# Second block of a four-layer model on one core: where the embedding sums go, how far the expert tiles are fetched ahead, when the router is split, and how the gate's bias is added

## The chip, the cores and the metric

The kernel runs on one core of one Trainium2 chip. The metric is the time of one execution on the device, in microseconds. Engines are called by their names: TensorE (PE in the rows, its weight loads PEld), VectorE (DVE), ScalarE (ACT), GpSimd (POOL) and SyncE (SP), which only issues DMAs here.

## What is computed

512 tokens of width 1024 pass two layers of a first block (not touched by the change) and two layers of a second one. A layer of the second block is, in the reference's own code:

```python
x = layer_norm(DEEPNORM_ALPHA * x + mix @ w_o[i], ln1_g[i], ln1_b[i])
ffn = expert_choice_moe(x, router_w[i], w1[i], w3[i], w2[i])
ple = jax.nn.sigmoid(x @ ple_gate_w[i] + ple_gate_b[i]) * (p[i] @ ple_w[i])
x = layer_norm(DEEPNORM_ALPHA * x + ffn + ple, ln2_g[i], ln2_b[i])
```

`expert_choice_moe` takes a softmax of `x @ router_w` over 16 experts; each expert picks its 64 best tokens, gathers their rows of x, computes `(silu(xg @ w1) * (xg @ w3)) @ w2`, weighs the result by the affinity and adds it to the token's row. One expert's three matrices are 1024x1024 floats each.

## The kernel before, in words

Products that need more than one rounded pass are written as three: an operand is split into `hi` (rounded to fp32r, by ScalarE) and `lo` (the rest, by VectorE), and `products` gives hi x hi, hi x lo, lo x hi. Some products stay whole in f32.

`gemm` is the stage that all projections use. It runs over weight tiles of 128x2048 floats (1 MB), four of which lie in a ring (`w_ring`); each is split into `pl_w_hi` and `pl_w_lo` in one of two homes, and each has its outputs, numbered k through the stage. A stage can have a `lead`, here the transposes of x into `xT` (32 on TensorE, then ScalarE's `xT_hi` and VectorE's `xT_lo`, eight each), and a `side`: work that each engine does ahead of its output k. Each engine runs its own list in order and waits on semaphores; a stage ends with a barrier of all engines.

A layer of the second block has, after its mixer, two stages:

- The embedding stage (`pl`, built by `ple_tiles`). Outputs 0 to 15 are the gate `x @ ple_gate_w`: four 1 MB tiles, each with four outputs of twelve products; a bank gets two of them, and at the end of the second (outputs 4 to 7 and 12 to 15) one more product adds the bias: row n of an identity, spread over 128 columns, times `pb`, whose two rows are the bias. ScalarE then writes the sigmoid into `pg`. Outputs 16 to 23 are `p @ ple_w`, six products each; VectorE multiplies by `pg` and scales x by 1.41 and adds to it, in two instructions. The side is `route_beside`, the routing. TensorE: logits ahead of output 1 (24 products with the split router `rws`), transposes ahead of 2, 4, 11 and 13, the gather of the first two experts' tokens ahead of 18 and 20. VectorE: the router's split (`split_router`) ahead of its output 0, softmax at 1, the top-64 search at 3 and 4, the places at 7. SP: router weights, an iota table, `pb`, six expert tiles into `ex_front`, and after the places the p rows, then the embedding weight. ScalarE copies x to `xs` at its output 0, because the gather reads it while VectorE changes x; VectorE waits for that at output 16.
- The experts stage (`experts`). Two experts are taken in one turn, eight turns of 24 tiles: 8 of w1, 8 of w3, 8 of w2. The tiles go round twelve slots, four of the ring, six of `ex_front`, two of `ex_back`; the last two belong to this stage alone, so SP fetches them at its start. After that SP refills a slot when TensorE is done with its tile. The first ten are there when the stage begins. Each expert's result is scattered by products, and VectorE adds it to x; the layer norm follows.

In `gemm`, VectorE's list begins so (ScalarE's has the same form), and it is here that the change moves an entry:

```python
split(0)
...
for n in range(len(tiles)):
    for m in ahead_of(n):
        split(m)
    for k in range(last[n] - len(outs_of[n]), last[n]):
        if side and k in side.dve:
            side.dve[k](dve, s)
```

so the second weight tile is split ahead of whatever the side does at output 0.

Of the kernel before, what the change touches and what calls it, by code (L numbers as in the profile page):

```python
# [44 lines left out]
DEPTH = 2  # L45

# [165 lines left out]
def gemm(nc, label, ps, ring, tiles, pre=0, nxt=(), lead=None, also=(), side=None, banks=NB):  # L212
# [10 lines left out]
    with ExitStack() as ctx:  # L223
# [43 lines left out]
        with stage(nc, label, f"{names} {side.names}" if side else names, clear=ready) as (block, s):  # L267
# [136 lines left out]
            def _(dve):  # L404
# [1796 lines left out]
def route_beside(nc, ctx, ps, C, x, xT, pt, pT, pb, I, iota, pos, aff_s, xs, E, i):  # L2201
# [7 lines left out]
    mx, work, top = sb("mx", [P, 3, TT]), sb("work", [NE, 2, T]), sb("top", [NE, 8, 8])  # L2209
# [5 lines left out]
    def sp(sp, s):  # L2215
# [3 lines left out]
        sp.dma_start(pb[:, :], I["ple_gate_b_2"][i].rearrange("(a n) -> a n", a=2)).then_inc(s.pb_in, 16)  # L2219
# [6 lines left out]
    def pool(pool, s):  # L2226
        pool.memset(ones[:, :], 1.0).then_inc(s.ones, 1)
# [4 lines left out]
    def bias_in(pe, s):  # L2232
        pe.wait_ge(s.pb_in, 16)
# [72 lines left out]
    def split_router(dve, s):  # L2306
# [3 lines left out]
        dve.tensor_tensor(rws.lo[:, :, :], rw[:, :, :], rws.hi[:, :, :].bitcast(F32), ALU.subtract).then_inc(s.rw_split, 1)  # L2310

# [81 lines left out]
def gather(pe, ps, bank, xs, E, j):  # L2393

    for t in range(TT):
        mm = pe.matmul(ps[:, bank + j // 4, j % 4 * P:j % 4 * P + P], xs[:, t, pairs_of(j)], E.sel_now[:, t, :], start=(t == 0), stop=(t == TT - 1))  # L2396
# [8 lines left out]
def experts(nc, ps, ring, C, w1, w3, w2, x, xs, iota, pos, aff_s, E, i, gain, bias, store=None, nxt=()):  # L2405
# [15 lines left out]
    with ExitStack() as ctx:  # L2421
        def sb(name, shape, dt=F32):
            return ctx.enter_context(sbuf(nc, f"{name}{i}", shape, dt))
        back = sb("ex_back", [P, BACK, SLOT])
# [14 lines left out]
        slots = RING + AHEAD + BACK  # L2439

        def slot(n):
            n = n % slots
            home, first = (ring.slots, 0) if n < RING else (E.front, RING) if n < RING + AHEAD else (back, RING + AHEAD)
# [15 lines left out]
        with stage(nc, f"ex{i}", names, clear=ready) as (block, s):  # L2459
# [5 lines left out]
            def _(sp):  # L2465
# [11 lines left out]
                for m in range(RING + AHEAD, slots):  # L2477
                    fetch(0, m)
# [35 lines left out]
            def _(pe):  # L2514
                def gather_next(js):
                    for j in js:
                        mm = gather(pe, ps, H1_BANK, xs, E, j)
# [82 lines left out]
            def _(act):  # L2600
# [25 lines left out]
                def total(t):  # L2626
                    act.wait_ge(s.added, (turns - 1) * SC + 2 * t + 2)
                    act.activation(junk[:, t, :], x[:, t, :], ACT.Copy, accum_out=col(SUM, t)).then_inc(s.n_sum, 1)
                total(0)
                for t in range(TT):  # L2630
# [3 lines left out]
                    act.activation(junk[:, t, :], x[:, t, :], ACT.Square, bias=col(LESS_MEAN, t), accum_out=col(SQUARES, t)).then_inc(s.n_squares, 1)  # L2634
# [4 lines left out]
            def _(dve):  # L2639
# [42 lines left out]
                def centre(t):  # L2682
                    dve.scalar_tensor_tensor(y[:, t, :], x[:, t, :], col(LESS_MEAN, t), rows[:, 0, :], ALU.add, ALU.mult).then_inc(s.n_less, 1)
# [18 lines left out]
def ple_tiles(I, i, xT, pT, pb, C, x, pg):  # L2702


    def gate(w, n, q, t):
# [6 lines left out]
        mm.append((C.ident[0:2, n:n + 1].broadcast_to([2, P]), pb[0][:, :]))  # L2712
        return out(P, 512, mm, bank=bank, first=False, **to(pg[0][:, t, cols], "A", 1.0, ACT.Sigmoid))

    def embed(w, hf, t):
        cols = slice(512 * hf, 512 * hf + 512)

        def v(e, p, st):
            g = pg[0][:, t, cols]
# [3 lines left out]
            return e.scalar_tensor_tensor(x[:, t, cols], x[:, t, cols], ALPHA, g, ALU.mult, ALU.add)  # L2723
# [7 lines left out]
def block2_layer(nc, ps, ring, C, x, I, i, store, nxt):  # L2731
    late = {n: [] for n in ("xT", "pT", "pb", "pg")}
    ple = ple_tiles(I, i, late["xT"], late["pT"], late["pb"], C, x, late["pg"])
# [12 lines left out]
    with ExitStack() as ctx:  # L2746
        def sb(name, shape, c=ctx):
            return c.enter_context(sbuf(nc, f"{name}{i}", shape, F32))

        xs = sb("xs", [P, TT, D])  # L2750
# [5 lines left out]
                  ready=[ctx.enter_context(nc.semaphore(f"ex{i}_ready{n}")) for n in range(AHEAD + BACK)], order=[I[n][i] for n in ("w1_2", "w3_2", "w2_2")])  # L2756
        with ExitStack() as c2:
            xT, pT = pair(nc, c2, f"xT{i}", [P, DC, T]), pair(nc, c2, f"pT{i}", [P, 2, T])
            pg, pb = sb("pg", [P, TT, D], c2), sb("pb", [2, 512], c2)
            for n, tensor in (("xT", xT), ("pT", pT), ("pg", pg), ("pb", pb)):  # L2760
# [111 lines left out]
```

## Time and profile before

| | us |
|---|---|
| median of three runs | 3378.24 |
| lowest and highest | 3373.71 and 3387.47 |
| the profiled execution, its own time | 3375.86 |
| its span, first to last instruction | 3374.1 |

The profile is that of one execution. Times in its rows count from the span's start. In the timeline a row gives start, duration, engine, line, operation, what it writes and reads, and in brackets how long the engine had been idle and what released it; "x4" is four instructions merged in one row. SPq rows are DMA issues. Layer 0 of the second block has its embedding stage from 1973.3 and its experts stage from 2066.2; in layer 1 these are 2798.7 and 2892.0.

### The profile page before, as it was taken

The numbers are of one execution on the slowest core, as the hardware profiler recorded it, in microseconds if no ns is written. First come the engines' busy times: TensorE is split into PE (matmuls) and PEld (weight loads), VectorE is DVE, ScalarE is ACT, GpSimd is POOL, SyncE is SP. The second block draws the span as 40 slices with busy tenths as digits, with TensorE's granted clock in tenths as the row PEclk, the third lists the DMA queues.
The fourth block names the chain that finished last, engine by engine and source line by source line (L and its number), as shares of the span: only waits on it lengthen the run. The fifth ranks groups of instructions, "written<-read, shape, count | busy, mean of one in ns | idle before, by whom it ended". The sixth has DMA issues, their size and how long they took to land. (4 is left out here: it accounts for less than half of the span.)

```text
span 3374.1 us, 39981 instructions
## 1 busy us (share of the span) xinstructions
PE 3186.6 (94%) x16110; PEld 2169.8 (64%) x16110; DVE 1285.4 (38%) x1773; ACT 957.7 (28%) x1570; POOL 236.3 (7%) x361
## 2 busy tenths in 40 slices
PE   7999999999999999999997999999988899999996
PEld 5886578888787667888785566444437456544442
DVE  4425554242532564334366462111116655111113
ACT  3325433142422633323343421010013543000001
POOL 1004200000100410000000200000000310000000
PEclk9998999999999999999998999999998999999998
DMA  5310123231441022323311136999992113799997
GB/s 159 119 56 26 63 82 99 95 99 63 131 138 38 1 88 88 100 89 99 91 37 43 68 119 254 426 427 426 427 415 64 58 63 134 303 426 427 427 427 303
DMA packets 234295, 590.22 MB, mean 175 GB/s; under 512 B 42962, under 2 KB 146328, under 8 KB 184996
## 3 DMA queue, kind: packets, MB, share of 16 engines
q1 hardware_dynamic: 234148, 588.15, 46.0%
q8 instruction: 105, 1.72, 0.2%
q14 instruction: 42, 0.34, 0.0%
HBM read 581.81 MB, written 2.10 MB: 173 GB/s over the span
## 5 line engine op out<-in xcount | busy, mean ns | idle before, releaser
L2576 PE MATMUL ps<-w_ring,xe 128*64 128x512 f32 x1024 | 233.8, 602 | 18.5 <-DMA w_ring<-in_w 13.4
L422 DVE TENSOR_TENSOR mlp_w_lo<-w_ring,mlp_w_hi 128x2048 fp32r<-128x2048 f32 x62 | 142.1, 2292 | 205.7 <-ACT mlp_w_hi L382 205.7
L357 PE MATMUL ps<-h_hi,in_w_hi 128*128 128x512 f32 (+1 forms) x528 | 206.9, 392 | 2.6 <-DVE h_lo L430 2.6
L357 PE MATMUL ps<-h_lo,in_w_hi 128*128 128x512 f32 (+1 forms) x528 | 205.6, 389 | 0.0
L357 PE MATMUL ps<-h_hi,in_w_lo 128*128 128x512 f32 (+1 forms) x528 | 205.6, 389 | 0.0
L357 PE MATMUL ps<-h_hi,mlp_w_hi 128*128 128x512 f32 x512 | 199.4, 389 | 2.0 <-DVE h_lo L430 2.0
L357 PE MATMUL ps<-h_hi,mlp_w_lo 128*128 128x512 f32 x512 | 199.2, 389 | 0.0
L357 PE MATMUL ps<-h_lo,mlp_w_hi 128*128 128x512 f32 x512 | 199.2, 389 | 0.0
L357 PE MATMUL ps<-mlp_w_lo,u_hi 128*128 128x512 f32 x512 | 199.2, 389 | 0.0
L357 PE MATMUL ps<-mlp_w_hi,u_hi 128*128 128x512 f32 x512 | 199.2, 389 | 0.0
L357 PE MATMUL ps<-mlp_w_hi,u_lo 128*128 128x512 f32 x512 | 199.2, 389 | 0.0
L382 ACT ACTIVATE mlp_w_hi<-w_ring 128x2048 fp32r<-128x2048 f32 x62 | 118.5, 1911 | 230.1 <-PE ps L357 230.1
L2576 PEld LDWEIGHTS ps<-w_ring,xe 128*64 128x64 f32 x1024 | 75.6, 138 | 164.5 <-issue 164.4
L2576 PE MATMUL ps<-ex_front,xe 128*64 128x512 f32 x768 | 174.4, 598 | 0.0
L2576 PE MATMUL ps<-ex_front,hidT 128*64 128x512 f32 x768 | 168.8, 594 | 2.5 <-ACT hidT L2616 2.2
L2667 DVE SCALAR_TENSOR_TENSOR ye_lo<-ps,g_now,ye_hi 128x1024 fp32r<-128x1024 f32 x16 | 20.5, 1284 | 354.1 <-ACT ye_hi L2622 354.1
L2647 DVE TENSOR_TENSOR x<-x,ps 128x512 f32<-128x512 f32 x128 | 82.2, 683 | 169.3 <-PE ps L2539 169.3
L422 DVE TENSOR_TENSOR in_w_lo<-w_ring,in_w_hi 128x2048 fp32r<-128x2048 f32 (+1 forms) x38 | 83.4, 2194 | 133.3 <-ACT in_w_hi L382 133.1
L2396 PEld LDWEIGHTS ps<-sel_now,xs 128*128 128x128 f32 x1024 | 123.5, 196 | 11.7 <-issue 11.4
L2396 PE MATMUL ps<-sel_now,xs 128*128 128x128 f32 x1024 | 127.2, 283 | 0.0
L700 ACT ACTIVATE w_ring<-ps,at_top 128x128 f32<-128x128 f32 (+1 forms) x192 | 99.2, 523 | 98.2 <-DVE at_top L757 98.0
L2576 PEld LDWEIGHTS ps<-ex_front,hidT 128*64 128x64 f32 x768 | 54.0, 137 | 105.3 <-issue 101.0
(551 smaller groups left out, 6146.1 us busy)
## 6 DMA issues: line engine op xcount, KB each, us to landing
ex_front<-in_w SPq DMA_DIRECT2D x192, 1024.0 KB, 17.4
w_ring<-in_w SPq DMA_DIRECT2D x128, 1024.0 KB, 20.5
ex_back<-in_w SPq DMA_DIRECT2D x64, 1024.0 KB, 19.7
w_ring<-in_w_in SPq DMA_DIRECT2D x32, 1024.0 KB, 5.4
w_ring<-in_w_up SPq DMA_DIRECT2D x32, 1024.0 KB, 5.4
w_ring<-in_w_down SPq DMA_DIRECT2D x32, 1024.0 KB, 5.0
w_ring<-in_cmp_w SPq DMA_DIRECT2D x16, 512.0 KB, 4.9
w_ring<-in_w_out SPq DMA_DIRECT2D x8, 1024.0 KB, 6.1
```

The lines of the kernel that those rows point to most:

```text
L357: mm = pe.matmul(ps[0:o.rows, bank[k], 0:o.cols], lhsT, rhs, start=(o.first and j == 0), stop=(o.final and j == len(o.mm) - 1))
L382: act.activation(w.hi[:, home(n), 0:used], ring.slots[:, n % RING, 0:used], ACT.Copy).then_inc(s.hi_done, 1)
L422: dve.tensor_tensor(w.lo[:, home(n), 0:used], ring.slots[:, n % RING, 0:used], w.hi[:, home(n), 0:used].bitcast(F32), ALU.subtract).then_i ...
L700: act.activation(probs[:, u % (LAG + 1), a, 0:n], ps[:, S_BANK + 2 * (u % 2) + a, 0:n], ACT.Exp, bias=top[:, u % 8, a:a + 1], accum_out=to ...
L2396: mm = pe.matmul(ps[:, bank + j // 4, j % 4 * P:j % 4 * P + P], xs[:, t, pairs_of(j)], E.sel_now[:, t, :], start=(t == 0), stop=(t == TT - 1))
L2576: mm = pe.matmul(ps[rows, bank + half, :], lhsT, slot(2 * m + a)[:, kk, 512 * half:512 * half + 512], start=(k == 0), stop=(k == DC - 1))
L2647: dve.tensor_tensor(d, d, ps[:, TR_BANK + n % 2 if bank is None else bank, :], ALU.add).then_inc(s.added, 1)
L2667: dve.scalar_tensor_tensor(ye.lo[:, :], ps[:, Y_BANK:Y_BANK + 2, :].rearrange("p b n -> p (b n)"), g_now[:, :], ye.hi[:, :].bitcast(F32), ...
```

## The change

`LEAD` is a new place in the side's list of VectorE: after the lead's remainders and before any further tile is split. `split_router` moves there. The bias becomes a product in fp32r: `pb` is now 128 rows, zeroed by GpSimd, with the rounded bias in rows 0 and 1 (ScalarE, `round_bias`) and what the rounding left in rows 32 and 33 (VectorE, `rest_of_bias`); the stationary side is a column of `marks`, the rounded form of a table that has ones in rows n, 32 + n, 64 + n and 96 + n. TensorE waits for it ahead of output 4. `pg` is gone: gates, embedding sums and the experts' adds use one buffer `acc`, so x stays as it was until the layer norm, the gather reads x, and `xs`, its copies and the wait for them go. `ex_back` is gone too: `ex_front` has eight tiles, all fetched in the embedding stage.

```diff
+LEAD = -1
@@ gemm, VectorE
+                if side and LEAD in side.dve:
+                    side.dve[LEAD](dve, s)
                 for n in range(len(tiles)):
@@ route_beside
-    mx, work, top = sb("mx", [P, 3, TT]), sb("work", [NE, 2, T]), sb("top", [NE, 8, 8])
+    mx, tables, top = sb("mx", [P, 3, TT]), sb("work", [P, 2, T]), sb("top", [NE, 8, 8])
+    work, pb_in = tables[0:NE, :, :], tables[HD:HD + LO + 2, 0, :]
...
-        sp.dma_start(pb[:, :], I["ple_gate_b_2"][i].rearrange("(a n) -> a n", a=2)).then_inc(s.pb_in, 16)
+        for r in (0, LO):
+            sp.dma_start(pb_in[r:r + 2, :], I["ple_gate_b_2"][i].rearrange("(a n) -> a n", a=2)).then_inc(s.pb_in, 16)
         for m in range(AHEAD):
...
+        pool.memset(pb[:, :].bitcast(F32), 0.0).then_inc(s.pb_zero, 1)
...
     def bias_in(pe, s):
-        pe.wait_ge(s.pb_in, 16)
+        pe.wait_ge(s.pb_lo, 1)
...
             if b == 0:
                 pe.wait_ge(s.selected, 1)
-                pe.wait_ge(s.x_kept, TT)
...
-                mm = gather(pe, ps, ROUTE_A, xs, E, j)
+                mm = gather(pe, ps, ROUTE_A, x, E, j)
...
-    def keep_x(act, s):
-        for t in range(TT):
-            act.activation(xs[:, t, :], x[:, t, :], ACT.Copy).then_inc(s.x_kept, 1)
+    def round_bias(act, s):
+        act.wait_ge(s.pb_in, 32)
+        act.wait_ge(s.pb_zero, 1)
+        for r in (0, LO):
+            ins = act.activation(pb[r:r + 2, :], pb_in[r:r + 2, :], ACT.Copy)
+        ins.then_inc(s.pb_hi, 1)
...
+    def rest_of_bias(dve, s):
+        dve.wait_ge(s.pb_hi, 1)
+        dve.tensor_tensor(pb[LO:LO + 2, :], pb_in[LO:LO + 2, :], pb[LO:LO + 2, :].bitcast(F32), ALU.subtract).then_inc(s.pb_lo, 1)
...
-    return beside(names, sp, {0: bias_in, 1: logits_by_expert, 2: logits_by_token, 4: affinities_by_expert, 11: places_by_token, 13: p_by_feature, 16: p_ready, 18: gather_half(0), 20: gather_half(1)},
-                  {0: keep_x, 3: exponentials, 14: round_p, 20: take_half(0), 22: take_half(1)},
-                  {0: split_router, 1: softmax, 3: take_top(0, 3), 4: take_top(3, 8), 7: places, 11: keep_places, 14: rest_of_p, 15: select_first, 16: x_is_kept}, pool)
+    return beside(names, sp, {1: logits_by_expert, 2: logits_by_token, 4: bias_and_affinities, 11: places_by_token, 13: p_by_feature, 16: p_ready, 18: gather_half(0), 20: gather_half(1)},
+                  {0: round_bias, 3: exponentials, 14: round_p, 20: take_half(0), 22: take_half(1)},
+                  {LEAD: split_router, 0: rest_of_bias, 1: softmax, 3: take_top(0, 3), 4: take_top(3, 8), 7: places, 11: keep_places, 14: rest_of_p, 15: select_first}, pool)
 
-AHEAD, BACK = 6, 2
+AHEAD = 8
@@ experts
-        slots = RING + AHEAD + BACK
+        slots = RING + AHEAD
...
-                for m in range(RING + AHEAD, slots):
-                    fetch(0, m)
                 with sp.Fori(0, turns - 1) as it:
@@ ple_tiles
-        mm.append((C.ident[0:2, n:n + 1].broadcast_to([2, P]), pb[0][:, :]))
-        return out(P, 512, mm, bank=bank, first=False, **to(pg[0][:, t, cols], "A", 1.0, ACT.Sigmoid))
+        mm.append((C.marks[:, n:n + 1].broadcast_to([P, P]), pb[0][:, :]))
+        return out(P, 512, mm, bank=bank, first=False, **to(acc[0][:, t, cols], "A", 1.0, ACT.Sigmoid))
...
-            return e.scalar_tensor_tensor(x[:, t, cols], x[:, t, cols], ALPHA, g, ALU.mult, ALU.add)
+            return e.scalar_tensor_tensor(g, x[:, t, cols], ALPHA, g, ALU.mult, ALU.add)
@@ block2_layer
-        xs = sb("xs", [P, TT, D])
+        acc = sb("acc", [P, TT, D])
...
-            pg, pb = sb("pg", [P, TT, D], c2), sb("pb", [2, 512], c2)
+            pb = c2.enter_context(sbuf(nc, f"pb{i}", [P, 512], F32R))
@@ build, the stage that rounds the tables at the start
-                for dst, src in ((C.ident_r[:, :], C.ident[:, :]), (C.later[:, :], tri), (C.cmp_neg[:, :, :], cmp)):
+                for dst, src in ((C.ident_r[:, :], C.ident[:, :]), (C.later[:, :], tri), (C.marks[:, :], C.heads), (C.cmp_neg[:, :, :], cmp)):
                     act.activation(dst, src, ACT.Copy).then_inc(s.copied, 1)
```

In the lists below, line numbers of the changed kernel are a few higher than before, since lines were added. VectorE, start of layer 0's embedding stage, before: the split of the first tile, the eight remainders of xT, the second tile, the router, the copy of the logits (into `p`) and the softmax's first steps.

```order
L414 TENSOR_TENSOR pl_w_lo<-w_ring,pl_w_hi 128x512 x4
L430 SCALAR_TENSOR_TENSOR xT_lo<-ps,xT_hi 128x512 x8
L422 TENSOR_TENSOR pl_w_lo<-w_ring,pl_w_hi 128x2048
L2308 CAST rws_hi<-rw_448 128x128
L2310 TENSOR_TENSOR rws_lo<-rw_448,rws_hi 128x128
L2315 COPY p_435<-ps 16x512
L2317 COPY lg_449<-ps 128x64
```

The same place in the changed kernel:

```order
L415 TENSOR_TENSOR pl_w_lo<-w_ring,pl_w_hi 128x512 x4
L431 SCALAR_TENSOR_TENSOR xT_lo<-ps,xT_hi 128x512 x8
L2316 CAST rws_hi<-rw_448 128x128
L2318 TENSOR_TENSOR rws_lo<-rw_448,rws_hi 128x128
L423 TENSOR_TENSOR pl_w_lo<-w_ring,pl_w_hi 128x2048
L2322 TENSOR_TENSOR pb_447<-work_451,pb_447 2x512
L2327 COPY p_436<-ps 16x512
L2329 COPY lg_449<-ps 128x64
```

The router's two instructions now stand ahead of the second tile's split, and the bias remainder stands between that split and the copy of the logits.

SP, from the bias of layer 0 to the first refill in the experts stage, before (the ISA and branch rows are the barrier and the stage's loop):

```order
L2219 DMA pb_447<-in_ple_gate_b 2x512
L2222 DMA ex_front_433<-in_w_2 128x2048 x6
L2224 DMA p_435<-in_p 128x4x256
L292 DMA w_ring<-in_ple_w 128x2x1024
L302 DMA w_ring<-in_w_2 128x2048 x4
L115 UNCONDITIONAL_BRANCH
L118 ISA x5
L2464 UNCONDITIONAL_BRANCH
L2470 DMA ex_back_498<-in_w_2 128x2048 x2
```

and in the changed kernel, where `work` is the buffer that also holds the bias as it arrives:

```order
L2224 DMA work_451<-in_ple_gate_b 2x512 x2
L2227 DMA ex_front_434<-in_w_2 128x2048 x8
L2229 DMA p_436<-in_p 128x4x256
L293 DMA w_ring<-in_ple_w 128x2x1024
L303 DMA w_ring<-in_w_2 128x2048 x4
L116 UNCONDITIONAL_BRANCH
L119 ISA x5
L2476 UNCONDITIONAL_BRANCH
```

Two expert tiles moved from the experts stage's start into the run of front tiles, and the bias is fetched twice.

ScalarE, the same start, before: two rounds of tile splits around the transposes of x, then the copies of x, then the exponentials.

```order
L372 ACTIVATE pl_w_hi<-w_ring 128x512 x4
L389 ACTIVATE xT_hi<-ps 128x512 x8
L382 ACTIVATE pl_w_hi<-w_ring 128x2048
L2295 ACTIVATE xs_432<-x 128x1024 x4
L2299 ACT_TABLE_LOAD
L2299 ACTIVATE lg_449<-lg_449 128x64
```

and in the changed kernel:

```order
L373 ACTIVATE pl_w_hi<-w_ring 128x512 x4
L390 ACTIVATE xT_hi<-ps 128x512 x8
L383 ACTIVATE pl_w_hi<-w_ring 128x2048
L2302 ACTIVATE pb_447<-work_451 2x512 x2
L2307 ACT_TABLE_LOAD
L2307 ACTIVATE lg_449<-lg_449 128x64
```

The four copies are replaced by the two roundings of the bias.

## Rows read from the trace of the kernel before

**Rows 1.** The page: span.

```profile
span 3374.1 us, 39981 instructions
```

**Rows 2.** Windows of both experts stages: busy time, then PEclk, DMA share, GB/s.

```profile
2066.20:2071.95 5.75, 5.53 (x18) 2.07 (x20) 0.00 (x0) 1.28 (x1) 0.19 (x1) 0.70 0.81 302
2071.95:2493.20 421.25, 416.33 (x2136) 189.16 (x2132) 60.83 (x93) 35.54 (x44) 2.46 (x13) 1.00 1.01 426
...
2940.00:3319.60 379.60, 374.22 (x1906) 168.14 (x1904) 58.61 (x89) 31.82 (x39) 2.09 (x11) 1.00 1.01 427
```

**Rows 3.** Timeline of layer 0's experts stage, SP and TensorE.

```profile
2066.22 0.80 SPq L2470 DMA_DIRECT2D ex_back<-in_w  x2
2071.95 4.32 SPq L2470 DMA_DIRECT2D w_ring<-in_w  x4
...
2518.18 3.65 PE L2576 MATMUL ps<-ex_back,hidT 128*64 128x512 f32 x16 [1.28 <-DMA ex_back<-in_w]
```

**Rows 4.** Timeline of layer 0, around the logits.

```profile
1976.41 4.87 DVE L430 SCALAR_TENSOR_TENSOR xT_lo<-ps,xT_hi 128x512 fp32r<-128x512 f32 x8
...
1981.50 0.39 PE L357 MATMUL ps<-pl_w_hi,xT_lo 128*128 128x512 f32 x1
...
1983.99 0.22 DVE L2308 CAST rws_hi<-rw 128x128 fp32r<-128x128 f32 x1
1984.24 0.29 DVE L2310 TENSOR_TENSOR rws_lo<-rw,rws_hi 128x128 fp32r<-128x128 f32 x1
...
1984.68 0.58 PE L2240 MATMUL ps<-xT_hi,rws_hi 128*16 128x512 f32 x1 [2.79 <-DVE rws_lo L2310]
...
1991.70 0.40 PE L357 MATMUL ps<-pl_w_hi,xT_hi 128*128 128x512 f32 x1
```

**Rows 5.** Timeline of layer 1, the same place.

```profile
2801.75 4.87 DVE L430 SCALAR_TENSOR_TENSOR xT_lo<-ps,xT_hi 128x512 fp32r<-128x512 f32 x8
...
2807.19 0.39 PE L357 MATMUL ps<-pl_w_hi,xT_lo 128*128 128x512 f32 x1
...
2810.30 0.39 PE L2240 MATMUL ps<-xT_hi,rws_hi 128*16 128x512 f32 x1 [2.73 <-DVE rws_lo L2310]
...
2817.41 0.40 PE L357 MATMUL ps<-pl_w_hi,xT_hi 128*128 128x512 f32 x1
```

**Rows 6.** Windows of TensorE alone: length, busy (instructions), granted clock, DMA share, GB/s.

```profile
1975.00:1977.00 2.00, 2.00 (x11) 0.50 0.81 158
...
1979.00:1981.73 2.73, 2.73 (x14) 1.00 1.02 429
...
1984.68:1988.01 3.33, 3.33 (x9) 0.51 1.02 431
1988.01:2003.80 15.79, 15.79 (x74) 1.00 0.20 85
```

**Rows 7.** Timeline of layer 0: gates on ScalarE, embedding sums on VectorE.

```profile
2012.91 0.60 ACT L467 ACTIVATE pg<-ps 128x512 f32<-128x512 f32 x1 [3.39 <-PE ps L357]
2016.90 0.60 ACT L467 ACTIVATE pg<-ps 128x512 f32<-128x512 f32 x1 [3.39 <-PE ps L357]
...
2062.58 0.69 DVE L2722 TENSOR_TENSOR pg<-ps,pg 128x512 f32<-128x512 f32 x1
...
2063.94 0.69 DVE L2722 TENSOR_TENSOR pg<-ps,pg 128x512 f32<-128x512 f32 x1
```

**Rows 8.** Timeline: ScalarE's copies, GpSimd's memset, a rounding at the program's start.

```profile
12.70 0.29 ACT L2789 ACTIVATE cmp_neg<-w_ring 128x128 fp32r<-128x128 f32 x1
...
1973.32 0.52 POOL L2227 MEMSET p<- 16x512 f32 x1 [65.73 <-POOLq L119]
...
1981.61 3.91 ACT L2295 ACTIVATE xs<-x 128x1024 f32<-128x1024 f32 x4
```

**Rows 9.** Timeline of layer 0: last step of the places, their transposes.

```profile
2018.47 0.42 DVE L2346 TENSOR_SCALAR work<-work 16x512 f32<-16x512 f32 x1
...
2025.18 0.42 PE L2258 MATMUL ps<-ident,work 16*128 16x16 f32 x4
```

More of the change, by code:

```diff
@@ L2390, in select, with gather @@
                              E.pos_now[:, :, :].unsqueeze(3).broadcast_to(shape), ALU.is_equal)
-def gather(pe, ps, bank, xs, E, j):
+def gather(pe, ps, bank, x, E, j):
     for t in range(TT):
-        mm = pe.matmul(ps[:, bank + j // 4, j % 4 * P:j % 4 * P + P], xs[:, t, pairs_of(j)], E.sel_now[:, t, :], start=(t == 0), stop=(t == TT - 1))
+        mm = pe.matmul(ps[:, bank + j // 4, j % 4 * P:j % 4 * P + P], x[:, t, pairs_of(j)], E.sel_now[:, t, :], start=(t == 0), stop=(t == TT - 1))
     return mm
@@ L2402, in take_rows, with experts @@
     return act.activation(E.xe[:, :, 4 * b:4 * b + 4, :], ps[:, bank + b, :].rearrange("p (j a c) -> p a j c", j=4, a=2), ACT.Copy)
-def experts(nc, ps, ring, C, w1, w3, w2, x, xs, iota, pos, aff_s, E, i, gain, bias, store=None, nxt=()):
+def experts(nc, ps, ring, C, w1, w3, w2, acc, x, iota, pos, aff_s, E, i, gain, bias, store=None, nxt=()):
     order = (w1, w3, w2)
@@ L2438, in experts @@
         ring.now ^= 1
-        slots = RING + AHEAD + BACK
+        slots = RING + AHEAD
         def slot(n):
             n = n % slots
-            home, first = (ring.slots, 0) if n < RING else (E.front, RING) if n < RING + AHEAD else (back, RING + AHEAD)
+            home, first = (ring.slots, 0) if n < RING else (E.front, RING)
             return home[:, n - first, :].rearrange("p (k n) -> p k n", k=2)
@@ L2516, in gather_next @@
                     for j in js:
-                        mm = gather(pe, ps, H1_BANK, xs, E, j)
+                        mm = gather(pe, ps, H1_BANK, x, E, j)
                         if j == DC - 1:
@@ L2633, in _ @@
                     act.wait_ge(s.n_mean, t + 1)
-                    act.activation(junk[:, t, :], x[:, t, :], ACT.Square, bias=col(LESS_MEAN, t), accum_out=col(SQUARES, t)).then_inc(s.n_squares, 1)
+                    act.activation(junk[:, t, :], acc[:, t, :], ACT.Square, bias=col(LESS_MEAN, t), accum_out=col(SQUARES, t)).then_inc(s.n_squares, 1)
                     act.wait_ge(s.n_squares, t + 1)
@@ L2682, in centre @@
                 def centre(t):
-                    dve.scalar_tensor_tensor(y[:, t, :], x[:, t, :], col(LESS_MEAN, t), rows[:, 0, :], ALU.add, ALU.mult).then_inc(s.n_less, 1)
+                    dve.scalar_tensor_tensor(y[:, t, :], acc[:, t, :], col(LESS_MEAN, t), rows[:, 0, :], ALU.add, ALU.mult).then_inc(s.n_less, 1)
                 def finish(t):
@@ L2699, in _, with ple_tiles @@
                     finish(t)
[L2702 removed]
+def ple_tiles(I, i, xT, pT, pb, C, x, acc):
     def gate(w, n, q, t):
@@ L2731, in block2_layer @@
 def block2_layer(nc, ps, ring, C, x, I, i, store, nxt):
-    late = {n: [] for n in ("xT", "pT", "pb", "pg")}
-    ple = ple_tiles(I, i, late["xT"], late["pT"], late["pb"], C, x, late["pg"])
+    late = {n: [] for n in ("xT", "pT", "pb", "acc")}
+    ple = ple_tiles(I, i, late["xT"], late["pT"], late["pb"], C, x, late["acc"])
     with ExitStack() as ctx:
@@ L2755, in block2_layer @@
         E = Names(front=front, xe=xe, sel_now=sel_now, pos_now=pos_now, aff_now=aff_now,
-                  ready=[ctx.enter_context(nc.semaphore(f"ex{i}_ready{n}")) for n in range(AHEAD + BACK)], order=[I[n][i] for n in ("w1_2", "w3_2", "w2_2")])
+                  ready=[ctx.enter_context(nc.semaphore(f"ex{i}_ready{n}")) for n in range(AHEAD)], order=[I[n][i] for n in ("w1_2", "w3_2", "w2_2")])
         with ExitStack() as c2:
             xT, pT = pair(nc, c2, f"xT{i}", [P, DC, T]), pair(nc, c2, f"pT{i}", [P, 2, T])
-            pg, pb = sb("pg", [P, TT, D], c2), sb("pb", [2, 512], c2)
-            for n, tensor in (("xT", xT), ("pT", pT), ("pg", pg), ("pb", pb)):
+            pb = c2.enter_context(sbuf(nc, f"pb{i}", [P, 512], F32R))
+            for n, tensor in (("xT", xT), ("pT", pT), ("acc", acc), ("pb", pb)):
                 late[n].append(tensor)
-            side = route_beside(nc, c2, ps, C, x, xT, pt, pT, pb, I, iota, pos, aff_s, xs, E, i)
+            side = route_beside(nc, c2, ps, C, x, xT, pt, pT, pb, I, iota, pos, aff_s, E, i)
             gemm(nc, f"pl{i}", ps, ring, ple, RING, expert_tiles(E.order),
                  flips(C, lambda i, j: x[:, i, j * P:(j + 1) * P], xT, halves=True), side=side, banks=ROUTE_A)
-        experts(nc, ps, ring, C, I["w1_2"][i], I["w3_2"][i], I["w2_2"][i], x, xs, iota, pos, aff_s, E, i, I["ln2_g_2"][i], I["ln2_b_2"][i], store, nxt)
+        experts(nc, ps, ring, C, I["w1_2"][i], I["w3_2"][i], I["w2_2"][i], acc, x, iota, pos, aff_s, E, i, I["ln2_g_2"][i], I["ln2_b_2"][i], store, nxt)
 def build(nc, I, result, sizes=None):
@@ L2778, in build @@
                   **{n: ctx.enter_context(sbuf(nc, n, shape, F32R)) for n, shape in
-                     (("ident_r", [P, P]), ("later", [P, 2 * P + HD]), ("cmp_neg", [P, TT, 32]))})
+                     (("ident_r", [P, P]), ("later", [P, 2 * P + HD]), ("cmp_neg", [P, TT, 32]), ("marks", [P, H1]))})
         tri, cmp = ring.slots[:, 0, 0:2 * P + HD], ring.slots[:, 1, 0:P].rearrange("p (t n) -> p t n", t=TT)
```

16 lines of the change are left out of this document (8 added, 8 removed).

## The prediction

> **What bounds the kernel now.** I read the page first, then the windows of the second block, then the timelines at the two ends of each layer's embedding stage. The profiled execution spans 3374.1 us [rows 1] and took 3375.86 us, so 1.8 us lie around the span; it is 2.4 us below the median of the three runs, 3378.24. Block one, most of the span, is not touched.
>
> Each layer of the second block has two stages that matter here, with two different limits. In the experts stage the windows show 426 and 427 GB/s with a DMA share of 1.01 from the first freed slot to the last issue [rows 2]: the weight stream sets the end there, although TensorE is busy for 416 of 421 us too. One tile (128x2048 floats, 1.049 MB) takes 1.049 / 427 = 2.46 us. The timeline gives the check: the first freed slot is refilled at 2071.95, 180 tiles are left of 192, 180 x 2.46 = 442 us, and the last wait for a tile ends at 2518.18, 446 us later [rows 3]; the 4 us over are the way in and out. So this stage's end is its first refill plus a constant. Anything that brings that first refill forward moves the end by as much, and nothing else in the stage does.
>
> In the embedding stage before it TensorE is the chain. It stands still once, for 2.79 us in layer 0 and 2.73 us in layer 1, ahead of the first logits product [rows 4, 5], and it pays eight bias products per layer. Both lie before the first refill, so both pass through to the end.
>
> **Router split early.** Before, VectorE does eight xT remainders until 1976.41 + 4.87 = 1981.28, then the whole split of the second weight tile, and only then the router's two instructions, 1983.99 to 1984.53; TensorE's last product of the first output starts at 1981.50 and the logits wait until 1984.68 [rows 4]. After, the two instructions follow the remainders: 1981.28 + 0.56 = 1981.84, with the same 0.15 us from end to release 1981.99. Gain 2.69 us. In layer 1 the remainders end at 2806.62, the router at 2807.18, release 2807.33, but TensorE is free only one product (0.23 us) after 2807.19, at 2807.42; before it was 2810.30 [rows 5]. Gain 2.88 us. The tile's split starts some 0.1 us later; it is needed by the fifth output, over 10 us on.
>
> **The clock after the stall.** Behind the stall the granted clock is 0.51 for 3.33 us, the 1.2 GHz level; before it the clock had been 1.00 [rows 6]. The 24 logits products take 1991.70 - 1984.68 = 7.02 us in layer 0 and 2817.41 - 2810.30 = 7.11 in layer 1 [rows 4, 5]; at 0.23 us each they take 5.5. Without the stall I expect no fall: gain 1.5 and 1.6 us. Bounds: 0 (it falls all the same) and these. I take them, because the fall stands directly behind the only gap.
>
> **Bias as one rounded product.** Outputs with a bias follow each other at 2016.90 - 2012.91 = 3.99 us; outputs of six plain products at 2063.94 - 2062.58 = 1.36 us, 0.227 a product [rows 7]. Twelve products are 2.72 us, so the bias costs 1.27 us now. The new form, one rounded product with 128 rows that hold mostly zeros, is not in the trace. Below, it costs 0.227 us like its neighbours of that type and width; above, as much as now. I take 0.227, the row that it is nearest to. Gain 1.04 us each, eight per layer: 8.3 us, less 0.2 where transposes follow one of them: 8.1.
>
> The Trainium skill weighs it otherwise: FP8 and Floating Point Precision, section TensorE Precision Notes, says that a true FP32 product takes four passes through the array, which at 0.227 us a pass is 0.91 us now and a gain of 0.68 each. By that rule the layers give 5.4 us each here and the whole sum is 19.2, some 3357 us. The rows show 1.27, so 0.36 us beyond four passes, and the row decides.
>
> What feeds the new form. ScalarE rounds twice 2x512, at 0.60 each by the 128x512 row [rows 7], in the place where four copies of x held it for 3.91 us [rows 8]: hidden, ready near 1983. VectorE's remainder, about 0.6 us like one of the eight xT remainders [rows 4], runs behind the second tile's split, so from 1984.2 to 1984.8. TensorE asks for it only at the fifth output, near 1996; behind that wait would stand the affinities' transposes and all later outputs. The nearer danger is VectorE itself: in order behind that remainder stands the copy of the logits, due when the logits end, 1982.0 + 5.5 = 1987.5. Cover 2.7 us. GpSimd zeroes the bias buffer first, about 0.52 us like its present memset of 512 elements a partition [rows 8]; over by 1974. The added rounding of the marks at the program's start costs up to 0.29 us, the row of a 128x128 rounding there [rows 8]; I take 0.25 on the path, below 0, above 0.3.
>
> **No copy of x, sums into the gates' buffer.** The embedding's second instruction and the experts' adds write elsewhere, same number and shape: nothing. The four copies on ScalarE (3.91 us) go; they are over by 1985.5, and the first gather, which waited for them, comes behind all sixteen gate outputs. Nothing.
>
> **Twelve tiles ahead.** SP issues two more front tiles and one more bias row. Eight tiles are 19.7 us of transfer instead of 14.7, from about 1975 to 1995; the next loads in that queue are p and the embedding weight, behind the placing, which ends at 2018.89 before [rows 9] and near 2014.7 after. Hidden. What it removes are two loads at the experts' start, 2066.22, which move while TensorE works on tiles that have landed. At the first refill their 5.75 us at 302 GB/s have carried 1.74 of 2.10 MB [rows 2], so 0.36 MB, 0.85 us, is still in front of it. The gain is between 0 and 0.85 us a layer; I take 0, because in a window that starts with an empty queue the first refill has its own way in, which is longer.
>
> **What is late next.** The places on VectorE come 6.3 us before TensorE wants them (2018.89 and 2025.18) [rows 9]. Both come forward by 4.2 us; TensorE alone by four more bias products, 4.2 us. Cover left 2.1 us. So no new stall, but the smallest cover here.
>
> **Sum.** Layer 0: 2.7 + 1.5 + 8.1 = 12.3. Layer 1: 2.9 + 1.6 + 8.1 = 12.6. Less 0.25 at the start: 24.6 us. From the profiled 3375.86 that is 3351.2; from the median 3353.6. I forecast 3352.
>
> **Rivals.**
> *The clock falls all the same.* If the fall has another cause than the gap, the 1.2 GHz stretch stays: 24.6 - 3.1 = 21.5, some 3355 us. Against it: from 1975 to 1977 the clock is 0.50, from 1979 to 1981.73 it is 1.00, it came up while TensorE ran without a gap, and 0.51 stands directly behind the only gap [rows 6]. Chance 0.10.
> *A late bias.* The two bias rows go out just ahead of eight tiles in one queue. If they landed with them, near 1995, VectorE's copy of the logits would slip from 1987.5 to about 1997, and with it the chain to the places, which has 2.1 us of cover: 5 to 8 us a layer lost, 3362 to 3368. It starts to count from a landing at 1987.5 - 0.6 - 1.2 = 1985.7. For it: the queue is shared. Against: the rows go out first, and the router's weights, issued one step earlier, did not hold up anything. Any other lost cover on that chain gives the like. Chance 0.14.
> *The head start counts.* If the refills began two tiles earlier in effect, 2 x 2.46 = 4.9 us a layer more: 3342. Against: the same 180 tiles are left at the first refill in both kernels. Chance 0.06.
> *Slower.* The place is the run of gate products behind the logits. Had the clock stayed at 1.2 GHz there, each us of work would become two; from 12.3 us of such work in a layer on, the gain is gone, and over the seven outputs of 2.72 and eight of 2.95 us behind the logits, 42.6 us, it would give 30 us a layer back: 3436 us. For it: the clock did fall here once. Against: it was back at 1.00 from 1988.01 on [rows 6]. Chance 0.03.
> *My forecast*, 3347 to 3358: chance 0.67.
>
> **Numbers.** A measurement of this kernel tells about 0.5% from no change, 17 us. The forecast, the clock rival and the head start are all faster by more, with a small part of the late bias: 0.84. The rest of the late bias is within 0.5%: 0.12. Slower, with what I have not thought of: 0.04. The range goes from the head start to the late bias, 3342 to 3367; it leaves out the slower case and the edges of these two.
>
> **What would show it.** Right: no wait of TensorE ahead of the logits above 0.3 us, granted clock 1.00 through them, bias outputs 2.95 us apart, the first refill 12 us earlier after the stage's start, windows still at 427 GB/s. Wrong: a wait of VectorE's logits copy or of the bias remainder on ScalarE or DMA; a bias product of over 0.4 us to the next; a TensorE wait on the places; or an experts stage that is longer from first refill to last tile than 446 us.

## The result and the profile after

The changed kernel takes 3358.86 us, median of five runs (3351.57 to 3360.13); the kernel before, with two runs more, 3379.51. The ratio is 0.9943, 95% interval 0.9925 to 0.9961: 0.6% faster, 7 us above the forecast of 3352, 1 us above the band of 3347 to 3358 that it gave its chance of 0.67, and inside the range. The profiled execution took 3355.72 us; the page gives its span:

```profile
span 3353.9 us, 39952 instructions
```

Against [rows 1] that is 20.2 us less. The pieces, from the starts of the stages and the two rows of TensorE and SP that the prediction used:

| piece | before | after | difference |
|---|---|---|---|
| start to layer 0's embedding stage | 1973.32 | 1967.14 | -6.18 |
| embedding stage to the experts' first product, layer 0, 1 | 93.09, 93.51 | 80.59, 80.90 | -12.50, -12.61 |
| first product of the experts to first refill | 5.54, 5.54 | 4.16, 3.86 | -1.38, -1.68 |
| first refill to last wait for a tile | 446.23, 446.26 | 452.29, 453.43 | +6.06, +7.17 |
| the rest | | | +0.92 |

The second line is what was forecast (12.3 and 12.6). The lines above and below it were not.

First the line that came true. TensorE's timeline in layer 0, last product of the first output, first two and last of the logits, next output:

```profile
1975.34 0.39 PE L358 MATMUL ps<-pl_w_hi,xT_lo 128*128 128x512 f32 x1
1975.71 0.39 PE L2246 MATMUL ps<-xT_hi,rws_hi 128*16 128x512 f32 x1
1975.94 0.40 PE L2246 MATMUL ps<-xT_lo,rws_hi 128*16 128x512 f32 x1
...
1981.03 0.40 PE L2246 MATMUL ps<-xT_hi,rws_lo 128*16 128x512 f32 x1
1981.27 0.40 PE L358 MATMUL ps<-pl_w_hi,xT_hi 128*128 128x512 f32 x1
```

The wait of [rows 4] is gone: the logits start 0.37 us behind the product ahead of them and take 5.56 us, not 7.02. TensorE's windows there (length, busy, granted clock, DMA share, GB/s) show no fall, where [rows 6] had 0.51:

```profile
1973.00:1975.71 2.71, 2.71 (x13) 1.00 1.01 426
1975.71:1981.27 5.56, 5.56 (x26) 1.00 1.01 421
```

VectorE's timeline shows the bias remainder without a wait, the logits copy waiting for TensorE alone, and later the end of the places; TensorE's shows their transposes:

```profile
1977.92 0.68 DVE L2322 TENSOR_TENSOR pb<-work,pb 2x512 fp32r<-2x512 f32 x1
1981.47 0.68 DVE L2327 COPY p<-ps 16x512 f32<-16x512 f32 x1 [2.86 <-PE ps L2246]
...
2008.04 0.42 DVE L2358 TENSOR_SCALAR work<-work 16x512 f32<-16x512 f32 x1
```

```profile
2010.65 0.41 PE L2264 MATMUL ps<-ident,work 16*128 16x16 f32 x4
```

The bias was not late, and the places keep 2.2 us of cover (2010.65 - 2008.46; forecast 2.1). ScalarE's gates, where [rows 7] had 3.99 us between outputs, are 2.96 to 2.97 apart:

```profile
1996.65 0.60 ACT L470 ACTIVATE acc<-ps 128x512 f32<-128x512 f32 x1 [2.37 <-PE ps L358]
1999.61 0.60 ACT L470 ACTIVATE acc<-ps 128x512 f32<-128x512 f32 x1 [2.37 <-PE ps L358]
```

The next product starts 0.24 us behind the bias product; behind its neighbours it is 0.23:

```profile
1996.21 0.40 PE L358 MATMUL ps<-pb,marks 128*128 128x512 f32 x1
1996.45 0.39 PE L358 MATMUL ps<-pl_w_hi,xT_hi 128*128 128x512 f32 x1
```

Now the two lines below it. The windows of both experts stages, columns as in [rows 2]; the last two stretches are the way from the first product to the first refill:

```profile
2051.89:2473.14 421.25, 411.92 (x2108) 187.28 (x2105) 60.55 (x91) 34.93 (x43) 2.46 (x13) 1.00 1.01 419
2920.00:3298.00 378.00, 367.37 (x1868) 166.06 (x1864) 58.16 (x89) 30.69 (x38) 2.09 (x11) 1.00 1.01 421
2047.73:2051.89 4.16, 4.16 (x20) 1.75 (x22) 0.00 (x0) 1.09 (x1) 0.01 (x1) 1.00 0.00 0
2866.44:2870.30 3.86, 3.86 (x18) 1.58 (x20) 0.00 (x0) 1.28 (x1) 0.01 (x1) 1.00 0.03 6
```

The share of the DMA engines is 1.01 as before, but they move 419 to 421 GB/s in place of 426 to 427: the same bytes, 1.4% slower, and TensorE does less in the same time (411.92 against 416.33 us). The timeline of SP and of TensorE has the two ends of it, as [rows 3]:

```profile
2051.89 3.99 SPq L2482 DMA_DIRECT2D w_ring<-in_w  x4
```

```profile
2504.18 3.65 PE L2586 MATMUL ps<-ex_front,hidT 128*64 128x512 f32 x16 [1.34 <-DMA ex_front<-in_w]
```

180 tiles x 1.049 MB / 421 GB/s = 448.5 us, and the 4 us of way in and out make 452.

### The profile page after: what moved, and what is told of

It is laid out like the page before. It is cut to its first block and busy times, and to the rows that moved or that the text cites. A ratio compares the mean times of both kernels' runs of the same rounds, so it can differ in the third digit from the quotient of the medians.

```text
span 3353.9 us, 39952 instructions
## 1 busy us (share of the span) xinstructions
PE 3160.3 (94%) x16094; PEld 2165.4 (65%) x16094; DVE 1287.2 (38%) x1775; ACT 952.5 (28%) x1567; POOL 237.4 (7%) x363
## 5 line engine op out<-in xcount | busy, mean ns | idle before, releaser
L2586 PE MATMUL ps<-ex_front,xe 128*64 128x512 f32 x1024 | 232.9, 598 | 0.0
L2586 PE MATMUL ps<-ex_front,hidT 128*64 128x512 f32 x1024 | 224.1, 594 | 5.9 <-DMA ex_front<-in_w 3.7
L2586 PEld LDWEIGHTS ps<-ex_front,hidT 128*64 128x64 f32 x1024 | 72.6, 137 | 145.4 <-issue 141.1
L2586 PEld LDWEIGHTS ps<-ex_front,xe 128*64 128x64 f32 x1024 | 70.1, 136 | 127.0 <-issue 126.7
L2657 DVE TENSOR_TENSOR acc<-acc,ps 128x512 f32<-128x512 f32 x128 | 82.6, 684 | 170.0 <-PE ps L2549 169.9
L2409 PEld LDWEIGHTS ps<-sel_now,x 128*128 128x128 f32 x1024 | 123.6, 197 | 11.6 <-issue 11.4
L2409 PE MATMUL ps<-sel_now,x 128*128 128x128 f32 x1024 | 127.3, 283 | 0.0
```

The lines of the kernel that those rows point to most:

```text
L2586: mm = pe.matmul(ps[rows, bank + half, :], lhsT, slot(2 * m + a)[:, kk, 512 * half:512 * half + 512], start=(k == 0), stop=(k == DC - 1))
L2657: dve.tensor_tensor(d, d, ps[:, TR_BANK + n % 2 if bank is None else bank, :], ALU.add).then_inc(s.added, 1)
```

## The experiments

**Is it the execution or the program?** The two kernels again, unchanged, and the changed kernel with the old split of the slots, all on one chip.

> The kernel before once more, unchanged, with a profile of its own. Two theories on why the weight stream moved 426 and 427 GB/s in the two experts stages before and 419 and 421 after. Variation: the rate belongs to the execution; this profile then shows a rate that may lie anywhere from 419 to 427, and block one (start to the embedding stage of layer 0) may take 1967 to 1974 us. Placement: the changed kernel's slots and order of loads cost the 1.5%; this profile then shows 426 to 427 in both layers and, as the first turn of both attention stages is the same code, about 1973 us for block one. Time: 3374 to 3388 by both.

> The changed kernel once more, unchanged. Variation: rate of the experts stages anywhere from 419 to 427 GB/s, the same in range as in the other kernels of this chip, block one 1967 to 1974 us. Placement: 419 to 421 again, in both layers, block one near 1967. Time 3351 to 3361 by both. The embedding stages, from their first instruction to TensorE's first product of the experts, 80.6 and 80.9 us by both.

```diff
-AHEAD = 8
+AHEAD, BACK = 6, 2
@@ experts
+        back = sb("ex_back", [P, BACK, SLOT])
...
+                for m in range(RING + AHEAD, slots):
+                    fetch(0, m)
```

> The changed kernel with six tiles ahead in ex_front and two in ex_back that are fetched at the start of the experts stage, as before. Variation: rate as in the other runs of this chip, and the time within 2 us of the changed kernel's, because the 180 tiles behind the first refill are the same; the first refill comes no more than 0.9 us later after the stage's start. Placement: the rate returns to 426 or 427 GB/s, the stage from first refill to last wait for a tile takes 446 us in place of 453, and the time falls by 12 to 13 us to some 3346.

The windows of the kernel before, then of the changed one, then of six and two:

```profile
2120.00:2470.00 350.00, 344.97 (x1771) 157.21 (x1768) 53.17 (x79) 30.18 (x37) 2.08 (x11) 1.00 1.01 427
```

```profile
2120.00:2470.00 350.00, 340.79 (x1750) 155.98 (x1748) 51.89 (x78) 29.06 (x36) 2.08 (x11) 1.00 1.01 421
```

```profile
2120.00:2470.00 350.00, 339.08 (x1740) 155.20 (x1736) 50.87 (x77) 29.06 (x36) 2.08 (x11) 1.00 1.01 421
```

The rate belongs to the program: variation falls. The split of the slots is not its cause either: six and two keeps 421, against what placement expected of it.

The head start of the two tiles is not worth nothing, though, as the prediction had put it. Six and two starts its refills no later (84.7 us behind the stage's start in both layers; 84.75 in layer 0 of the changed kernel), but the two tiles are then in front of them:

```profile
2051.39:2055.55 4.16, 4.16 (x20) 1.74 (x22) 0.00 (x0) 1.09 (x1) 0.01 (x1) 1.00 0.79 268
```

4.16 us at 268 GB/s have carried 1.11 of 2.10 MB; 0.98 MB, 2.3 us at 421 GB/s, are left, where the prediction counted 0.85 us from a refill that came 5.54 us behind the first product. From the start of the embedding stage to the last wait for a tile six and two takes 538.78 and 538.98 us, the changed kernel beside it 536.93 and 538.43: 1.85 and 0.55 us for the head start. (In layer 1 the changed kernel's first products ran at the lower clock here; beside the first profile's 538.19 it is 0.79.)

Block one does belong to the execution. GpSimd's first softmax product behind the zeroing of `att`, in the first and the second profile of the same changed kernel, each with the window between these two rows:

```profile
1769.62 0.95 POOL L1710 MEMSET att<- 128x1024 f32 x1 [14.19 <-POOLq L120]
1851.27 1.51 POOL L751 TENSOR_SCALAR mla_probs<-mla_probs,mla_inv,ones 128x512 f32<-128x512 f32 x2 [80.70 <-DVE mla_inv L773]
1769.62:1851.27 81.65, 62.90 (x317) 44.60 (x318) 55.41 (x120) 26.60 (x43) 0.95 (x1) 0.83 0.19 53
```

```profile
1774.82 0.95 POOL L1710 MEMSET att<- 128x1024 f32 x1 [14.18 <-POOLq L120]
1864.96 1.52 POOL L751 TENSOR_SCALAR mla_probs<-mla_probs,mla_inv,ones 128x512 f32<-128x512 f32 x2 [89.19 <-DVE mla_inv L773]
1774.82:1864.96 90.14, 69.97 (x317) 50.73 (x318) 55.63 (x120) 26.61 (x43) 0.95 (x1) 0.77 0.18 48
```

One stage of one program differs by 8.5 us: the same 317 products of TensorE take 69.97 us at a mean granted clock of 0.77, and 62.90 at 0.83. Layer 0's embedding stage starts at 1967.14 in one, at 1980.86 in the other. Over all profiles here it starts from 1966.16 to 1980.86 in versions of the changed kernel and from 1969.55 to 1973.32 in those of the kernel before, so the 6.18 us of the first table are of this kind. The changed kernel's eleven runs here go from 3352.97 to 3372.94, with a median of 3364.81, above the expected 3351 to 3361. Ratios of whole times therefore say less than the stretches in the profiles.

**Where the slots lie.** Buffers are laid one behind the other in the order in which the code makes them. The new `marks`, 8 columns or 32 bytes a partition, stands ahead of `acc` and `ex_front` and moves them: `ex_front` starts at byte 69920 of a partition in the changed kernel, at 69888 before. Two edits, one on each kernel; where `marks` is wider, here and below, the same eight columns are used and the rest lies idle:

```diff
-("marks", [P, H1])
+("marks", [P, 2 * H1])
```

> The changed kernel with marks as 16 columns, 64 bytes a partition, of which the first 8 are used; before it was 8 columns, 32 bytes. Everything that is allocated behind marks starts 32 bytes later: ex_front at byte 69952 of a partition, a multiple of 64, in place of 69920, which is not; in the kernel before it was 69888, a multiple of 64 as well. Address theory: the eight ex_front slots lie across 64-byte boundaries in the changed kernel and their transfers run slower for it. Then the experts windows return from 421 to 426 or 427 GB/s, the stretch from first refill to last wait for a tile from 452 to 454 us to 446 in both layers, and the kernel is 12 to 14 us faster than the changed one. Rival, the buffers' new use (gather reads x, adds go to acc) slows the stream: 421 GB/s and 452 us stay. Second rival, a coarser boundary (128 or 256 bytes) decides: the rate stays at 421 too, and the next run but one tells.

```diff
-("cmp_neg", [P, TT, 32])
+("cmp_neg", [P, TT, 32]), ("spare", [P, H1])
```

> The kernel before with an unused buffer of 8 columns, 32 bytes a partition, behind cmp_neg, where the change puts marks; nothing reads or writes it. ex_front then starts at byte 69920 and ex_back at 130208, as 69888 and 130176 before. Address theory: the experts windows fall from 427 to 421 GB/s, the stretch from first refill to last wait from 446 to 452 to 454 us in both layers, the time grows by 12 to 15 us; embedding stages unchanged (98.6 and 99.1 us from their start to the first refill). Rival, the buffers' use or the change's other edits: 427 GB/s, 446 us, the time of the kernel before within its spread.

The windows of the kernel before with 32 unused bytes:

```profile
2120.00:2470.00 350.00, 340.85 (x1751) 155.54 (x1749) 51.91 (x78) 29.09 (x36) 2.10 (x11) 1.00 1.01 421
```

An unused buffer takes the kernel before from 427 to 421 GB/s, from 446.45 to 452.14 us in layer 0 and from 446.36 to 451.91 in layer 1, and to a ratio of 1.0043 (1.0028 to 1.0058). So the 32 bytes alone, without any other edit of the change, cost 5.7 and 5.6 us. But 64 bytes do not mend the changed kernel: 422 GB/s, 451.45 us. The boundary is coarser. Three more layouts, and the changed kernel beside the first two on their chip:

```diff
+("marks", [P, 32])
```

> The changed kernel with marks as 32 columns, 128 bytes a partition, of which 8 are used. ex_front starts at byte 70016, a multiple of 128 and not of 256; the ring, at 1152, is the same in this. Address theory with a boundary of 128 bytes: 426 or 427 GB/s, 446 us from first refill to last wait in both layers, 12 to 14 us faster than the changed kernel. With a boundary of 256 bytes or more: 421 or 422 GB/s, 450 to 452 us, no faster than the changed kernel.

```diff
+        sb("spare", [P, 32])
         ring = Ring(nc, ctx)
...
+("marks", [P, 32])
```

> The changed kernel with marks of 128 bytes and an unused buffer of 128 bytes a partition ahead of the ring: the ring starts at byte 1280, ex_front at 70144, both multiples of 256, where in the kernel before only ex_front was one (ring 1152, ex_back 130176). Boundary of 128 bytes: as in the run beside it, 426 or 427 GB/s and 446 us, nothing more. Boundary of 256: all twelve slots gain, the rate goes beyond the 427 of before, in which six of twelve were on it, to some 430 or more, and the stretch falls below 446 us; the time is at least 13 us below the changed kernel's.

> The changed kernel beside these two on the same chip: 421 GB/s and 452 to 454 us from first refill to last wait in both layers by all theories; the time is the base that the two padded kernels are held against.

```diff
+        sb("spare", [P, 32])
         ring = Ring(nc, ctx)
...
+("marks", [P, 64])
```

> As the run with everything on 256 bytes, but marks are 256 bytes a partition: the ring starts at byte 1280, a multiple of 256, ex_front at 70272, 128 bytes past one. Of twelve slots four are on the boundary; none was at 422 GB/s, six at 427, twelve at 427 to 428. If every slot off the boundary costs its part, the rate lies between, at 424 to 426 GB/s, 447 to 450 us from first refill to last wait. If only the addresses of ex_front count, 422 GB/s and 451 us, no faster than the changed kernel. If the ring's address is what counts, 427 and 446 us, and the address theory as put here falls, since the ring did not move when the rate did.

Windows with marks of 128 bytes, with all on 256, with the ring alone on it:

```profile
2120.00:2470.00 350.00, 341.24 (x1752) 155.86 (x1750) 51.49 (x79) 29.06 (x36) 2.08 (x11) 1.00 1.01 422
```

```profile
2120.00:2470.00 350.00, 345.62 (x1772) 157.38 (x1770) 53.17 (x80) 30.11 (x37) 2.10 (x11) 1.00 1.01 427
```

```profile
2120.00:2470.00 350.00, 343.80 (x1766) 156.71 (x1762) 52.11 (x79) 29.09 (x36) 2.10 (x11) 1.00 1.01 425
```

All runs of this part and the next by the bytes by which ring, `ex_front` and `ex_back` (where there is one) start past a multiple of 256, as they follow from the sizes and the order of the buffers; layer 0 from first refill to last wait; time against the kernel before on the same chip:

| kernel | bytes past 256 | slots on 256 | GB/s | us | ratio |
|---|---|---|---|---|---|
| before again | 128, 0, 128 | 6 of 12 | 427 | 446.45 | 1.0 (0.9984 to 1.0016) |
| before + 32 bytes | 128, 32, 160 | 0 | 421 | 452.14 | 1.0043 (1.0028 to 1.0058) |
| after again | 128, 32 | 0 | 421 | 452.18 | 0.9967 (0.9950 to 0.9983) |
| after, third | 128, 32 | 0 | 421 | 452.20 | 0.9970 (0.9954 to 0.9986) |
| router late (below) | 128, 32 | 0 | 421 | 452.22 | 0.9975 (0.9958 to 0.9991) |
| six and two | 128, 32, 160 | 0 | 421 | 454.04 | 0.9955 (0.9937 to 0.9972) |
| marks 64 bytes | 128, 64 | 0 | 422 | 451.45 | 0.9970 (0.9956 to 0.9984) |
| f32 bias (below) | 128, 64 | 0 | 422 | 452.02 | 1.0008 (0.9995 to 1.0021) |
| f32 bias, router late (below) | 128, 64 | 0 | 422 | 452.34 | 1.0044 (1.0026 to 1.0062) |
| marks 128 bytes | 128, 128 | 0 | 422 | 451.31 | 0.9944 (0.9924 to 0.9965) |
| ring alone on 256 | 0, 128 | 4 of 12 | 425 | 448.11 | 0.9938 (0.9920 to 0.9955) |
| all on 256 | 0, 0 | 12 of 12 | 427 | 445.48 | 0.9922 (0.9904 to 0.9939) |

The rate rises with the number of slots on a multiple of 256 bytes; the expectation of 430 for all twelve was too high, since beyond six little more comes. Each of these edits moves other buffers too, so look inside one kernel. A round of twelve tiles, 29.6 us, is four of the ring and eight of `ex_front`. One round with the ring alone on 256, cut in halves from 2.5 us behind the first refill on, so that the four ring tiles fall into the first half:

```profile
2233.18:2247.99 14.81, 14.81 (x76) 5.62 (x72) 1.38 (x4) 0.60 (x1) 0.38 (x2) 1.00 1.01 428
2247.99:2262.79 14.80, 14.80 (x102) 10.62 (x102) 1.22 (x1) 2.11 (x3) 0.00 (x0) 1.00 1.01 423
```

Over thirteen rounds in each layer the first halves have 425 to 429 GB/s (mean 427.2), the second 421 to 424 (422.9). Cut alike, the changed kernel has means of 421.7 and 420.2, the one with all on 256 has 427.2 and 427.2. So the rate follows the slot that is being written, and not the layout of the whole. A boundary of 512 is not needed either: 69888 before and 1280, where the ring alone on 256 starts, are odd multiples of 256. The slots are not independent, though: in the kernel before, the half with the four ring tiles, all off the boundary, still has 425.8 (the other 427.2). This fits six aligned slots being worth almost as much as twelve; what carries the rate over to neighbours, and what sets the 427, no run shows. The time of marks with 128 bytes alone would have misled: its median (3353.56, six runs) is 12 us below the changed kernel's beside it, as the 128-byte theory expected, while its stream shows no change. The version with all on 256 beats both kernels: 3346.01 us beside 3365.32 for the changed one and 3372.31 before, same chip. 13.4 of these 19 us are in the stretches from first refill to last wait (452.20 to 445.48 us and 452.07 to 445.36).

**The terms of the sum.** The router split put back, and, with marks of 64 bytes, the old bias, then both:

```diff
-{LEAD: split_router, 0: rest_of_bias, ...
+{0: split_router_and_bias, ...
```

> The changed kernel with the router split back behind the second weight tile (the bias remainder right behind it). My theory of the two terms, stall and clock: TensorE waits 2.7 to 2.8 us ahead of the first logits product in both layers, the granted clock behind it falls to about 0.5 for some 3.3 us and costs 1.5 us more, so each embedding stage is 4.2 us longer and the whole 8 to 9 us slower than the changed kernel. Rival, the clock falls by another cause or not at all: the stall costs 2.7 us a layer alone, 5 to 6 us in all, with the clock at 1.00 behind it.

```diff
@@ ple_tiles; the fetch, the zeroing and the rounding of pb go back in the same way
-        mm.append((C.marks[:, n:n + 1].broadcast_to([P, P]), pb[0][:, :]))
+        mm.append((C.ident[0:2, n:n + 1].broadcast_to([2, P]), pb[0][0:2, :]))
```

> The changed kernel, marks padded to 64 bytes, with the bias as before: one f32 product of two rows of the identity with the bias, no rounding passes, no zeroing, one fetch. My term for the bias, 1.04 us for each of eight outputs less 0.2: bias outputs 3.99 us apart in place of 2.97, each embedding stage 8.1 us longer than in the padded kernel, 16.2 us in all. Rival, four passes only (0.91 us against 0.227): 5.4 us a layer, 10.9 in all, bias outputs 3.63 apart.

> The changed kernel, marks padded to 64 bytes, with the bias as before and the router split back behind the second tile: what is left of the change is acc in place of pg, xs and the copies, and eight tiles in ex_front. My terms: nothing. From the start of the embedding stage to the first refill 98.6 and 99.1 us as in the kernel before, within 0.5 us, and the time within 2 us of the kernel before. Rival, the tiles ahead or the freed ScalarE count: the first refill comes 0.85 us or more earlier in each layer, to 1.5 if what was left over in the experts' start (4.2 and 3.9 us from its start to the first refill against 5.5) is theirs and not the clock's.

TensorE's timeline with the router late, then its windows behind the stall:

```profile
1977.54 0.59 PE L2246 MATMUL ps<-xT_hi,rws_hi 128*16 128x512 f32 x1 [2.79 <-DVE rws_lo L2318]
```

```profile
1977.54:1980.86 3.32, 3.32 (x8) 0.51 1.02 429
1980.86:1984.57 3.71, 3.71 (x17) 1.00 1.02 417
2800.35:2803.58 3.23, 3.23 (x8) 0.53 1.01 426
```

Stall and fall come back together in both layers; the third window is layer 1's. From the stage's start to the experts' first product this kernel takes 84.86 and 84.61 us, 4.27 and 3.71 more than the changed one; the logits take 7.03 and 6.94 in place of 5.56. My theory holds; the rival, a stall without the fall, does not. In layer 1 less is lost because TensorE reached the logits 0.6 us sooner there. The median, 3364.71 beside 3364.81, does not show the expected 8 to 9 us: block one's spread is larger.

With the f32 bias, ScalarE's gates:

```profile
2000.98 0.60 ACT L470 ACTIVATE acc<-ps 128x512 f32<-128x512 f32 x1 [3.40 <-PE ps L358]
2004.98 0.60 ACT L470 ACTIVATE acc<-ps 128x512 f32<-128x512 f32 x1 [3.40 <-PE ps L358]
```

Outputs are 4.00 us apart, the stage takes 88.78 and 88.86 us, 8.14 and 8.08 more than with marks of 64 bytes alone (80.64 and 80.78): the forecast 8.1, and not the 5.4 of four passes. The ratio is 1.0008 (0.9995 to 1.0021). With both back, the way to the first refill is 98.62 and 98.98 us, as before (98.63 and 99.05): `acc`, the dropped copies and the tiles ahead are worth nothing there. Nor are they by the last wait for a tile, 550.96 and 550.26 us from the stage's start, where the kernel before with 32 unused bytes has 550.74 and 550.94. With its slots off the boundary that kernel is slower than before, 1.0044 (1.0026 to 1.0062); my expectation of its time had missed that.

## Why the prediction was right, and where it was not

- *Router split early, the clock behind it.* Right in cause and size: the wait is gone, the clock stays at 1.00, and the undo brings 2.79 us and 1.4 to 1.5 us back in each layer.
- *Bias as one rounded product.* Right: 4.00 - 2.97 = 1.03 us an output, against 1.04; undone, 8.1 us a layer. The row decided rightly against the rule of four passes that the prediction set beside it, by which 5.4 would have come.
- *Late bias, places.* Neither was late; the cover at the places was 2.2 us.
- *Marks at the start.* About 0.1 us, as the last rounding there moved from 12.70 to 12.84 while the first one moved from 12.12 to 12.17; forecast 0.25.
- *Tiles ahead, copies.* The copies: nothing, as forecast. The tiles ahead: nothing where the first refill comes 5.54 us behind the first product, as in the kernel before; in the changed kernel, where it comes sooner, 1.85 and 0.55 us against 0, the first of them above the bound of 0.85.
- *What failed.* The sentence that the sums "write elsewhere, same number and shape: nothing", and with it the step that the stage's end is "its first refill plus a constant". Number and shape were the same, but the prediction looked at no addresses and took the 427 GB/s over: 32 bytes of `marks` moved all six aligned slots off a multiple of 256 bytes. The stretch grew by 6.1 and 7.2 us; the 32 bytes alone cost 5.7 and 5.6. The prediction's own sign for it, a stretch longer than 446 us, is what showed it.
- *Not foreseen.* The first expert products ran at clock 1.00 in both layers, where [rows 2] had 0.70: the first refill came 1.4 and 1.7 us sooner. In layer 1 hardly any of it reached the end: from the embedding stage's start to the last wait the first profile takes 538.19 us there, the two others of the changed kernel, with the clock at 0.73, 538.43 and 538.30. Over all profiles, the ten starts with the f32 bias were all low; with the rounded one all nine of layer 0 were full and five of nine in layer 1, behind 2.5 to 2.6 us of idle time in either form. What decides it stays open.

So it was in part luck that the time fell into the range, with errors against each other: 13.2 us lost in the stream, against 3.1 us at the experts' start and 6.2 us of block one's own variation gained. The first comparison's 0.9943 flatters the change; beside the two later ones, 0.9967 and 0.9970, both within the 0.5% that the prediction put down as no change, and the stretches of the second block (-28.2 + 13.2 = -15.0 us), some 10 to 15 us are the change's.

## What to carry to other kernels

Where a stage is bound by a stream of weights, look at where each slot starts before counting a new small buffer as free: here 32 bytes in front of the slots cost 11 us in two layers, and starting all slots on multiples of 256 gave the changed kernel 13. A term that is nothing by the rows of the kernel before need not be nothing behind the other edits: the two tiles ahead gained only once the refill came sooner. When a kernel's time varies by 20 us between executions, read an edit of 5 to 15 us from the stretch that it touches. An undone edit in the final kernel tells a term more sharply than the ratio of the whole.

## What the runs showed of the hardware

- 8 KB rows into a partition at 421 to 422 GB/s when the slots start 32, 64 or 128 bytes past a multiple of 256, 427 when six or twelve of twelve start on one, 425 with four, and then 427.2 in the half of a round that holds these four and 422.9 in the other. The Trainium skill, DMA: Bandwidth & Descriptors, section How a descriptor splits into AXI transactions, has transactions of 256 bytes that start at multiples of 256, told of reading; these runs show the 256 on the written side. By its count of beats an 8192-byte row would take 257 in place of 256 at 32 bytes past and 260 at 128, so 0.4% and 1.6% as an estimate; the runs show 1.4% (421 against 427) and 1.2% (422), nearly the same for both, and so disagree with the count.
- A gap of 2.73 to 2.79 us in TensorE's work ahead of the logits was followed by a granted clock of 0.51 to 0.54 over 3.2 to 3.3 us, the lower of its two levels (1.2 GHz), before and with the router late, in layer 0 and layer 1; without the gap the clock stayed at 1.00. Behind the 2.51 to 2.60 us ahead of the experts it fell in 14 of 28 starts, to a mean of about 0.7 up to the first refill.
